# Another fixed order of the experts in a mixture-of-experts loop, and a table that says when the first two overflow blocks may load their weights

## The reference, cut to what matters

```
def _swiglu(x, wg, wu, wd):
    return (jax.nn.silu(x @ wg) * (x @ wu)) @ wd
...
    def run(a):
        xblk, e = a
        return _swiglu(xblk, w_eg[e], w_eu[e], w_ed[e])
...
    return (routed + shared).reshape(Bn, L, Dm)
```

## Time and profile before

| | |
|---|---|
| median of 3 runs | 2295.53 us (2287.34 to 2300.07) |
| the profiled execution, its own time | 2296.46 us |
| its span, first to last instruction | 2294.7 us |
| mean granted TensorE clock | 0.886 of full speed |
| TensorE matmuls busy | 1948.6 us, 85% of the span |
| HBM read and written | 329.43 MB and 57.07 MB |

### The profile page before, as it was taken

The page is one execution under the profiler, slowest core; times in us unless marked ns, Lnnn a source line. Parts: engine busy times, 40 slices in busy tenths (PEclk is TensorE's granted clock), DMA queues, the critical chain, the costliest instruction groups (busy, mean ns, idle before and its releaser), DMA issues.

```text
span 2294.7 us, 25257 instructions
## 1 busy us (share of the span) xinstructions
PE 1948.6 (85%) x8864; PEld 1003.1 (44%) x8864; DVE 874.5 (38%) x2367; ACT 470.4 (20%) x899; POOL 244.4 (11%) x187
## 2 busy tenths in 40 slices
PE   3579899999988888979978989999999998895560
PEld 1146555554456664335555434444444443342230
DVE  4843711002255553222236334434443333331138
ACT  0121102210055551130143111111111111110021
POOL 0000001000000000120000012122221212110114
PEclk7779657899989998989988999999999999997775
DMA  8921003000211003521016189999999998885563
GB/s 292 362 49 51 3 0 116 1 1 0 78 23 56 1 1 94 183 101 55 0 42 154 44 299 323 350 356 348 354 346 350 368 355 297 284 310 202 207 214 124
DMA packets 98489, 389.72 MB, mean 170 GB/s; under 512 B 26879, under 2 KB 29603, under 8 KB 68780
## 3 DMA queue, kind: packets, MB, share of 16 engines
q1 hardware_dynamic: 79356, 318.89, 37.3%
q0 software_dynamic: 19008, 69.21, 11.5%
HBM read 329.43 MB, written 57.07 MB: 168 GB/s over the span
## 4 chain that ended last, share of the span: by engine, by line
PE 42%; DMA 5%; issue 5%; DVE 3%; ACT 1%; POOL 0%; SPq 0%; POOLq 0%; DVEq 0%; ACTq 0%
PE psum L1001 20%; PE psum L1012 9%; PE psum L857 5%; DMA arena<-in_w_exp_up 5%; PE psum L982 3%; DVE arena L1676 1%; PE psum L891 1%; PE psum L1019 1%; PE psum L885 1%; PE psum L898 1%; PE psum L881 1%; DVE arena L1687 1%; PE psum L836 0%; DVE arena L1677 0%; DVE arena L1675 0%
## 5 line engine op out<-in xcount | busy, mean ns | idle before, releaser
L1001 PE MATMUL psum<-arena 128*32 128x512 f32 (+2 forms) x2016 | 481.4, 613 | 85.5 <-DMA arena<-in_w_exp_up 84.3
L1001 PEld LDWEIGHTS psum<-arena 128*32 128x32 f32 (+2 forms) x2016 | 175.1, 143 | 338.4 <-issue 328.2
L1012 PE MATMUL psum<-arena,tail 128*32 128x512 f32 (+2 forms) x1000 | 231.6, 595 | 0.0
L1626 DVE TENSOR_TENSOR arena<-arena,psum 128x256 f32<-128x256 f32 x65 | 39.5, 607 | 442.6 <-ACT arena L1945 439.6
L2069 POOL DMA_INDIRECT moe_rows<-arena x64 | 101.6, 1588 | 681.8 <-DVE arena L1654 313.3
L1945 ACT ACTIVATE arena<-psum 128x256 f32<-128x256 f32 x65 | 24.9, 383 | 547.7 <-PE psum L1001 547.7
L705 PE MATMUL psum<-arena 128*128 128x512 f32 (+1 forms) x384 | 126.2, 492 | 0.0
L1012 PEld LDWEIGHTS psum<-arena,tail 128*32 128x32 f32 (+2 forms) x1000 | 79.9, 138 | 105.3 <-issue 105.3
L857 PE MATMUL psum<-arena 128*128 128x512 f32 (+1 forms) x288 | 124.3, 593 | 0.9 <-ACT arena L1871 0.5
L746 PE MATMUL psum<-arena 128*128 128x512 f32 (+2 forms) x192 | 86.6, 567 | 10.4 <-ACT arena L1801 10.4
L857 PEld LDWEIGHTS psum<-arena 128*128 128x128 f32 (+1 forms) x288 | 68.6, 239 | 55.3 <-issue 40.1
(11 more groups left out here) (478 smaller groups left out, 2474.9 us busy)
## 6 DMA issues: line engine op xcount, KB each, us to landing
arena<-in_w_exp_gate SPq DMA_DIRECT2D x66, 1024.0 KB, 13.3
arena<-in_w_exp_up SPq DMA_DIRECT2D x66, 1024.0 KB, 16.3
arena<-in_w_exp_down SPq DMA_DIRECT2D x66, 1024.0 KB, 18.3
arena<-in_w_ada SPq DMA_DIRECT2D x12, 2048.0 KB, 8.7
arena<-in_w_ada_final SPq DMA_DIRECT2D x4, 2048.0 KB, 7.8
arena<-in_cache_k SPq DMA_DIRECT2D x32, 256.0 KB, 3.6
arena<-in_cache_v SPq DMA_DIRECT2D x32, 256.0 KB, 2.9
arena<-moe_rows SPq DMA_DIRECT2D x16, 512.0 KB, 10.1
```

The costliest lines, as they stand in the source:

```text
L1001: ins = pe.matmul(slot[2 + par][lo:hi, :].rearrange("p (u n) -> p u n", u=2), xTs[:, par, k, lo:hi], gu, start=(k == 0), stop=(k == KD - 1))
L1012: ins = pe.matmul(slot[1][lo:hi, n * 512:(n + 1) * 512], hTs[:, k, lo:hi], ring[:, at, 2, k * D + n * 512:k * D + (n + 1) * 512], start=(k ...
```

## The change

Three things change.

- The order of the items. The single items of 8 lanes are set aside and come last. Of the others, those with more rounds than experts, those with fewer, and those with as many are each spread evenly over the whole, and merged. By lanes the new order is

```
-    order, rounds, ahead = [], [], 0
-    while items:
-        it = min(items, key=lambda it: (abs(ahead + length(it) - len(it) - 1), len(it) if len(order) % 2 else -len(it), CAPS[it[0]]))
-        items.remove(it)
-        ahead += length(it) - len(it)
+    last = [it for it in items if len(it) < length(it) and len(it) == 1]
+    rest = [it for it in items if it not in last]
+    spread = []
+    for sign, shift in ((1, 0.2), (-1, 0.7), (0, 0.5)):
+        same = [it for it in rest if (length(it) > len(it)) - (length(it) < len(it)) == sign]
+        spread += [((i + shift) / len(same), it) for i, it in enumerate(same)]
+    order, rounds = [], []
+    for it in [it for _, it in sorted(spread)] + last:
...
+            dlink(ts(release_f, iota_row[0:1, :], float(NR + 1), None, ALU.add))
+            for q in range(2):
+                ins = dve.memset(release_f[:, q:q + 1], float(LAST_ROUND[E - RING + q] + 3))
+            dlink(ins)
+            dlink(cp(release_i, release_f))
...
                     e = sp.value_load(expert_i[0:1, bass.ds(j * 2 + q, 1)], min_val=0, max_val=E - 1)
-                    sp.wait_ge(down_done, j * 2 + (NR + q + 1))
+                    release = sp.value_load(release_i[0:1, bass.ds(j * 2 + q, 1)], min_val=3, max_val=NR + MAXBLK)
+                    sp.wait_ge(down_done, release)
                     load_expert(e, q)
+            sp.wait_ge(down_done, n_pairs * 2 + (NR + 1))
             sp.sem_inc(ld_gu[0], 32)
```

More of the change, by code:

```diff
@@ L113 @@
 LAST_ROUND = [max(b for b, gs in enumerate(ROUNDS) if any(g[2] == k for g in gs)) for k in range(E)]
-assert NR % 2 == 0 and LAST_ROUND[E - RING] <= NR - 2
+assert NR % 2 == 0 and LAST_ROUND[E - RING] <= NR - 2 and LAST_ROUND[E - RING + 1] <= NR - 1
 def col_tiles(b):
@@ L380, in hymba_program @@
         row_off = arena(35780, 4)
+        release_f = arena(35784, P, parts=1)
+        release_i = arena(35912, P, parts=1).bitcast(I32)
         row_all = arena(36064, NR + MAXBLK)
```

## The result

The changed kernel takes 2317.22 us (median of 4 runs, 2312.77 to 2322.3), against 2297.8 for the kernel before in the runs beside it: a ratio of 1.0101, 95% interval 1.0077 to 1.0125 (the two medians alone give 1.0085, inside it). It is slower by about 1%; the forecast was 2317, that is 22.1 us or 0.96% more than before. The profiled execution is the longest of the four, 2322.3 us with a span of 2320.5.

What follows compares the result with a forecast made beforehand. TensorE and DMA were taken as nearly matched, with early release of loads deciding. Loop 758.8 + 94.3 (waits) + 33.6 (clock) + 0.5 = 887.2 against 865.1 us, 22.1 longer, so a median of 2317 us; range 2300 to 2334.

Steps and rivals of the forecast that it cites:

- rounds without waits: Loop of rounds at TensorE's own pace, no load waited for: 758.8 us, 0.2 less than before.
- six waits of slack 0: Rounds 6, 18, 28, 37, 47, 56: load released with no round to cover it; 8.05 us each, 48.3 in all.
- five of the second-of-two kind: Rounds 17, 27, 36, 46, 55: second of two loads released together, one round of cover; 8.0 us each, 40.0.
- round 10: Round needing two loads, with two and one rounds of cover, behind a queue: wait of 6 us, bounds 3 and 9.
- behind the waits: Slow matmuls after each of twelve waits as TensorE's clock throttles: 2.8 us each, 33.6 in all.
- last wait: SyncE must see down(62) end before the surplus gate_up(64): 0.5 us, bounds 0 and 2.
- The count of slack: Rounds between a load's release and the gate_up needing it; explained eight old waits, predicted twelve new ones, 94.3 us.
- rounds 7, 29, 38, 48 and 57: Second of two loads with one round of cover, right behind another wait: claimed to cost nothing, by 2 us.
- The tail: End of the loop: the eight old waits go, overflow loads released by down(57); gain 106.1 us.
- "same" case: Rival: the loop's new waits are there but small, time 2291 to 2306 us; chance 0.12.
- The faster one: Rival: second of two loads arrives in time, five waits and their clock loss go, 54 us, 2263; chance 0.08.
- "worse" case: Rival: loads bunch behind waits, five more waits of 1 to 6 us with clock loss, 25 us, 2342; chance 0.09.

Runs made afterwards that it cites:

- e7: Changed kernel with another item order, no load without a round of cover, starting with two-expert rounds: 2227.93 us, ratio 0.971.
- e1: Changed kernel with the old release of the overflow loads, at the ends of down in rounds 60 and 61: 2346.42 us, ratio 1.0221.
- e4: Changed kernel, but for two loads released together SyncE issues gate and up of both before the two down matrices: 2306.68 us, ratio 1.0041.
- e6: Changed kernel with another item order, put together so that the count gives three long waits: 2227.29 us, ratio 0.9695.
- e8: Changed kernel with an order picked for few waits, plus gate and up of both loads issued before the down matrices: 2214.97 us, ratio 0.9648.
- e3: Changed kernel with 52 surplus 128 x 128 matmuls on TensorE ahead of each of the twelve waits: 2331.05 us, ratio 1.0155.
- e5: Changed kernel with 30 surplus 128 x 128 matmuls on TensorE ahead of each of the twelve waits: 2301.39 us, ratio 1.0023.

## Why the prediction was right

By its own steps, with what each term measured in the profiled execution of the changed kernel ("behind the waits" is the rest of the sum):

| term | forecast, us | measured, us |
|---|---|---|
| rounds without waits | 758.8 | 760.1 |
| six waits of slack 0 | 48.3 | 49.4 |
| five of the second-of-two kind | 40.0 | 44.3 |
| round 10 | 6 | 8.2 |
| behind the waits | 33.6 | 30.4 |
| last wait | 0.5 | 0 |
| loop | 887.2 | 892.3 |

The first line is higher because the first step took 1346.22 - 1334.46 = 11.8 us and not 10.50, with the first `gate_up` at 9.77; the other 63 steps are counted as forecast, and "behind the waits" is what is then left of 892.3, 2.5 a wait. The twelve `gate_up` rows by themselves show 26.6 of these 30.4.

**The count of slack.** It named all twelve rounds and no other, rounds 7, 29, 38, 48 and 57 did not wait, and it has since named the long waits of three more orders, but for the 5.56 us at the start of e7. This was the step that carried the forecast. That these waits are the cause is shown from three sides: two waits put back (e1), five shortened by what was queued ahead of them (e4), nine or more taken away (e6 to e8), each near the time that the count gives them. One kind of wait the count does not settle by itself: that of a round that starts two experts of slack 2 and 1, as rounds 10 here, 45 before, 34 in e6 and 52 in e7. In e6 rounds 4, 6, 8, 10, 12, 14, 17 and 20 start two experts of the same slack and wait 0.44 us at most. For this kind the queue of loads ahead has to be looked at too, and "nothing left over" in the prediction said too much.

**The second-of-two waits.** The term was too low by 4.3 us, and three of the five (9.68, 9.14, 9.28) lie above the upper bound of 9.0. The term is a sum of three, the issue of the second up matrix behind the release (2.5 us), its landing (16.2 to 18.6), and the 12.1 that TensorE has work for. The landings were inside their bounds, 17.1, 17.9, 18.3, 18.4 and 18.4 us; TensorE had work for 12.3. What lay outside was the issue, taken from one place: it came 2.7, 2.7, 3.5, 2.8 and 3.1 us behind the release. In the longest of these waits, at round 36, SyncE spent 1.39 us on the issue of one up matrix, where the other four took 0.4 to 0.65. The release finds the load before still under way there: its down matrix, issued at 1793.6, lands 23.3 us later at 1816.9, behind the release at 1814.1. That this is what held up SyncE is not shown, and it does not order the five waits: at round 27 the load before landed 3.0 us behind the release and the wait was 8.45, at round 46 it was 0.8 and 9.14.

```profile
1814.54 1.39 SPq L2251 DMA_DIRECT2D arena<-in_w_exp_up  x1
...
L2251 SPq DMA_DIRECT2D arena<-in_w_exp_down x1: 618/618/618, 1793.6 to 1793.6; - x1
DMA to landing us min/median/max: 23.3/23.3/23.3
...
L2251 SPq DMA_DIRECT2D arena<-in_w_exp_up x1: 677/677/677, 1817.6 to 1817.6; - x1
DMA to landing us min/median/max: 18.3/18.3/18.3
```

**Round 10.** Taken from round 45 of before (5.62), it measured 8.19, within its bounds. Four loads were released in the two rounds ahead of its own two (at the ends of `down(4)` and `down(5)`), against one a round before round 45; that this deeper queue makes the difference is likely and not tested.

**The clock.** Right in its mechanism, which was an inference from rows then and is shown now (e3, e5), and 0.3 us a wait too dear on average. The rule of the Trainium skill that spoke against the change (TensorE: Matmul & The Clock Gate, section HAM oscillation) held: twelve waits of 8 us paid the clock twelve times.

**The tail.** All that it was said to give it gave: no wait from round 57 on.

**The table and the last wait.** The table's three groups of instructions on VectorE (0.21, 0.07 and 0.22 us) lie ahead of an idle stretch that is still 14.58 us long, against 15.10. The last wait costs nothing: the step to the surplus `gate_up` is 11.70 us, as a single round's always is.

```profile
1283.45 0.21 DVE L1541 TENSOR_SCALAR arena<-tail 1x128 f32<-1x128 f32 x1
1283.72 0.07 DVE L1543 MEMSET arena<- 1x1 f32 x2
1283.82 0.22 DVE L1545 CAST arena<-arena 1x128 int32<-1x128 f32 x1
...
1305.77 0.29 DVE L1573 COPY tail<-psum 128x128 f32<-128x128 f32 x1 [14.58 <-PE psum L968]
```

**The median.** The loop was 5 us longer than forecast, and the median hit to the microsecond; the profiled execution, at 2322.3, is 5 us above the median. The agreement to the last digit is chance, and so is part of that of the loop: the waits and the first step came out 8.9 us dearer than forecast, the clock and the last wait 3.7 cheaper. By the medians the change cost 19.4 us where 22.1 were forecast. Two small slips of the prediction change nothing: the sum of the "same" case, 22.1 - 7 - 6 - 3 - 10, takes off 3 us for slack 0 at its lower bound, which its words do not name, and 9 and 6 us added as independent bring the upper end of the forecast to 2328, not 2331.

**The rivals.** The faster one needed the second of two loads to land 9.6 us after its issue; it lands at 17.1 to 18.4. The estimate by the fit of the Trainium skill (DMA: Bandwidth & Descriptors, section Anatomy of one DMA), a wait of about 2 us there, is far off: the waits are 7.7 to 9.7. That section gives the fit for transfers that GpSimd issues, one at a time, and these loads are SyncE's. That gathers and additions share the DMA engines with them is seen in the trace; that they make the whole difference is not shown, as no run leaves them out. The "same" case had every term at its lower bound, and none is; of the drift of the "worse" case there is one wait for a load, 0.28 us.

What the change aimed at, spreading the rounds that use up two experts, is not what was wrong with the old order. It looked at the balance of rounds and experts; the waits come from single places where a slot comes free two rounds before it is needed, or two slots come free together three rounds before an item needs both. Each of the five spread 2/2 items made one of each: its own round waits for the second of its two loads (17, 27 and so on), and the round behind it for a load of slack 0 (18, 28 and so on).

## What to carry to other kernels

With a ring of buffers and a fixed schedule, write down for every load the step that frees its slot and the step that needs it, mark where a load has no step of cover, is the second of two with only one, or is one of two loads for the same step, with one or two steps of cover, behind a long queue, and multiply by the measured wait. Here that gave every long wait but one of five orders, of four of them before they were run; of the third kind it is a suspicion, since most such places did not wait. Order the work by that count and not by an average rate: the order alone turned a loss of 1% into a gain of 3% (e6), and with the order of issue 3.5% (e8). Where a few waits must stay, shorten the queue ahead of the transfer that ends them, and remember that each wait of 4.3 us or more cost TensorE its clock here as well.

## What the runs showed of the hardware that was not expected

- Surplus matmuls in place of idle time keep TensorE at 2.4 GHz through a wait: 6.94 us of them and an idle rest of 0.86 us kept `gate_up` at 7.13 us, while a rest of 3.09 us did not (8.83). The gain is 25.5 us of the loop over twelve waits and 16 us of the median, for work that computes nothing; over the three waits of e8 no gain can be told.
- One call of a 128 x 128 float32 matmul by a 128 x 128 float32 operand is two matmuls in the trace and takes 11.86 / 52 = 0.23 us, not the 0.13 us that I had taken from the transposes.
- With the DMA engines at a share of 0.98 in the loop of e8 TensorE waits long for only three loads of 66. A queue near full did no harm here where each load was released in time.
